# Prompt heads' suffix sums in two rounded parts, a second softplus buffer, and the last value pages in the key buffers

## The reference

```
z = q.k * DH_B**-0.5 + bias
log_stay = where(mask, log_sigmoid(-z), 0)            # minus the softplus of z
after    = suffix sum of log_stay over later keys, without the key itself
w        = where(mask, exp(log_sigmoid(z) + after), 0)
out      = w @ v
```

## Time and profile before

| | |
|---|---|
| runs | 1594.25, 1589.31, 1594.34 us, median 1594.25 |
| profiled execution | 1589.86 us, span 1588.2 us |
| PE busy | 1528.0 us, 96% of the span |
| PE weight loads | 1378.7 us, 87% |
| DVE busy | 1027.7 us, 65% |
| ACT busy | 684.5 us, 43% |
| attention turns | about 258 to 465 us |
| key and value pages | 128 each, 256 KB a page |
| mean TensorE clock | 0.99 of full speed |

### The profile page before, as it was taken

How to read it: one execution, slowest core, us unless ns; L and a number is a source line. 1 busy time by engine, 2 the same in 40 slices (tenths; PEclk the granted TensorE clock), 3 DMA queues, 4 the chain that set the end, 5 groups by cost and what they waited for, 6 DMA issues and landing times.

```text
span 1588.2 us, 31016 instructions
## 1 busy us (share of the span) xinstructions
PE 1528.0 (96%) x12126; PEld 1378.7 (87%) x12126; DVE 1027.7 (65%) x1768; ACT 684.5 (43%) x1029; POOL 94.7 (6%) x173
## 2 busy tenths in 40 slices
PE   7899999999989999999999899999999999999995
PEld 7788987444459999999999889998899999999995
DVE  5555565455553877776667755877758676776665
ACT  5222223645624653344343734354555534344343
POOL 0000002333230000000000000000000000000000
PEclk9999999999999999999999999999999999999997
DMA  5322228898871322222322311223422222222311
GB/s 186 111 74 86 84 72 304 303 353 324 313 277 54 98 88 82 96 69 100 106 79 96 100 57 54 91 100 113 140 80 81 89 83 95 91 71 102 106 54 58
DMA packets 50611, 195.26 MB, mean 123 GB/s; under 512 B 7405, under 2 KB 9614, under 8 KB 36690
## 3 DMA queue, kind: packets, MB, share of 16 engines
q1 hardware_dynamic: 35938, 139.49, 25.9%
q0 software_dynamic: 14576, 54.41, 9.1%
HBM read 182.19 MB, written 11.68 MB: 122 GB/s over the span
## 4 chain that ended last, share of the span: by engine, by line
PE 79%; DVE 11%; ACT 4%; DMA 3%; issue 2%; SPq 1%; POOLq 0%; POOL 0%; ACTq 0%; DVEq 0%
PE ps L333 17%; PE ps L335 16%; PE ps L334 16%; PE ps L738 5%; PE ps L737 5%; PE ps L736 5%; DMA kbuf<-in_k_cache_dram 3%; DVE wlo L322 2%; PE ps L1637 2%; ACT whi L318 1%; SPq L1616 1%; PE ps L1664 1%; PE ps L1872 1%; DVE s0b L2653 1%; PE ps L1830 1%
## 5 line engine op out<-in xcount | busy, mean ns | idle before, releaser
L333 PE MATMUL ps<-xhi,whi 128*128 128x280 f32 x1344 | 402.6, 300 | 23.4 <-DVE wlo L543 10.9
L335 PE MATMUL ps<-xhi,wlo 128*128 128x280 f32 x1344 | 393.7, 293 | 0.0
L334 PE MATMUL ps<-xlo,whi 128*128 128x280 f32 x1344 | 393.6, 293 | 0.0
L333 PE MATMUL ps<-dhi,whi 128*128 128x280 f32 x1024 | 298.4, 291 | 4.7 <-DVE pj L1052 2.9
L335 PE MATMUL ps<-dhi,wlo 128*128 128x280 f32 x1024 | 298.4, 291 | 0.0
L334 PE MATMUL ps<-dlo,whi 128*128 128x280 f32 x1024 | 298.1, 291 | 0.0
L322 DVE TENSOR_TENSOR wlo<-raw,whi 128x2048 fp32r<-128x2048 f32 x97 | 222.1, 2290 | 113.0 <-ACT whi L318 112.6
L318 ACT ACTIVATE whi<-raw 128x2048 fp32r<-128x2048 f32 x96 | 183.3, 1910 | 235.1 <-PE ps L335 201.3
L333 PEld LDWEIGHTS ps<-xhi,whi 128*128 128x128 f32 x1344 | 255.6, 190 | 32.9 <-issue 18.6
L334 PEld LDWEIGHTS ps<-xlo,whi 128*128 128x128 f32 x1344 | 255.5, 190 | 0.5
L335 PEld LDWEIGHTS ps<-xhi,wlo 128*128 128x128 f32 x1344 | 255.3, 190 | 0.0
(11 more groups left out here) (448 smaller groups left out, 2358.5 us busy)
## 6 DMA issues: line engine op xcount, KB each, us to landing
raw<-in_weights_dram SPq DMA_DIRECT2D x98, 1024.0 KB, 4.9
kbuf<-in_k_cache_dram SPq DMA_DIRECT2D x128, 256.0 KB, 5.3
vbuf<-in_v_cache_dram POOLq DMA_DIRECT2D x128, 256.0 KB, 8.5
s0b<-in_gla_in_dram POOLq DMA_DIRECT2D x4, 1024.0 KB, 5.1
out_dram<-s0b POOLq DMA_DIRECT2D x4, 1024.0 KB, 6.8
hT<-in_x_dram SPq DMA_DIRECT2D x2, 1120.0 KB, 9.1
out_dram<-pj POOLq DMA_DIRECT2D x2, 1120.0 KB, 8.9
hT<-in_x_dram POOLq DMA_DIRECT2D x2, 1120.0 KB, 13.6
```

Of the source, the lines that this page charges most:

```text
L333: pe.matmul(out, whi[:, par, t, :], hi, start=first, stop=False)
L334: pe.matmul(out, whi[:, par, t, :], lo, start=False, stop=False)
L335: return pe.matmul(out, wlo[:, par, t, :], hi, start=False, stop=last)
```

## The change

The suffix sums of a prompt head are done on two parts of the softplus: `sph`, rounded to the type `float32r`, made by ScalarE (`phi_act`), and `spl`, the rest `sp - sph` in the same type, made by VectorE (`plo_dve`). PE multiplies each part by the inclusive mask `incl` and by `onesr`, both in that type, with one matmul for every pair of key blocks; the block sums are gone. `sp` and `spl` get a second buffer in a free slot of the low weight parts, so `psp_dve` waits for the head before the last one (`a_v` starts at 1). `sph` lies in the place of `lz`. The last sample's 16 value pages are issued by SyncE into the key buffers (`load_last_v`) after the last `qk_pe`, and GpSimd's loop ends one set earlier; the reload of `hT` now waits for the last `pv_pe` (`v_used` at 36).

```diff
+        vlast = [at(f"vlast{g}", (o_hT, o_hT + GB, o_K2, o_raw)[g], [P, PG, 4 * P]) for g in range(4)]
-        incl = at("incl", o, [P, P]); o += 512
+        incl = at("incl", o, [P, P], f32r); o += 512
+        onesr = at("onesr", o_s + 1184 + 1024, [P, P], f32r)
-        lz = at("lz", o, [P, WA]); o += 4 * WA
-        sp = at("sp", o, [P, WA]); o += 4 * WA
+        lz = at("lz", o, [P, WA])
+        sph = at("sph", o, [P, WA], f32r); o += 4 * WA
+        sps = [at("sp0", o, [P, WA]), at("sp1", o_lo + SLAB * 4, [P, WA])]
+        spl = [at("spl0", o, [P, WA], f32r), at("spl1", o_lo + SLAB * 4, [P, WA], f32r)]; o += 4 * WA
...
+        def load_last_v(sp_, numbers):
+            sp_.wait_ge(S["k_used"], 36)
+            for a in range(PG):
+                for g in range(4):
+                    sp_.dma_start(vlast[a][:, g], page(v_cache, numbers[4 * a + g])).then_inc(KLD[a], 16)
...
-            dve.wait_ge(S["a_sp"], i * 2 + (j + 1))
-            blk = lambda k, q, n=1: sp[:, KOFF[k] + P * (q - k):KOFF[k] + P * (q - k + n)]
-            own.link(dve.tensor_tensor(T_[0], blk(2, 3), blk(3, 3), ALU.add))
-            dve.tensor_tensor(T_[1][:, P:2 * P], blk(1, 3), T_[0], ALU.add)
-            own.link(dve.tensor_tensor(T_[1][:, 0:P], blk(1, 2), blk(2, 2), ALU.add))
-            dve.tensor_tensor(T_[2][:, 0:P], blk(0, 1), blk(1, 1), ALU.add)
-            dve.tensor_tensor(T_[2][:, P:3 * P], blk(0, 2, 2), T_[1], ALU.add).then_inc(S["a_T"], 1)
+        def phi_act(act, i, j):
+            act.wait_ge(S["a_sp"], i * 2 + (j + 1))
+            for r, c in FULL:
+                act.activation(sph[r, c], sps[j % 2][r, c], ACT.Copy).then_inc(S["a_h"], 1)
+        def plo_dve(dve, i, j):
+            for n, (r, c) in enumerate(FULL):
+                dve.wait_ge(S["a_h"], i * 4 + (2 * j + n + 1))
+                dve.tensor_tensor(spl[j % 2][r, c], sps[j % 2][r, c], sph[r, c].bitcast(f32), ALU.subtract)\
+                   .then_inc(S["a_T"], 1)
...
+            for part, (t, ready) in enumerate(((sph, "a_h"), (spl[j % 2], "a_T"))):
+                cols = lambda k, q: t[:, KOFF[k] + P * q:KOFF[k] + WID[k]]
+                pe.wait_ge(S[ready], i * 4 + (2 * j + 1))
+                for k in range(3):
+                    b, c = ZB[k]
+                    if part == 0 and k == 2:
+                        pe.wait_ge(S[ready], i * 4 + (2 * j + 2))
+                    pe.matmul(ps[:, b, c:c + WID[k]], incl[:, :], cols(k, 0), start=part == 0, stop=False)
+                    for n in range(k + 1, 4):
+                        pe.matmul(ps[:, b, c + P * (n - k):c + WID[k]], onesr[:, :], cols(n, 0), start=False,
+                                  stop=part == 1 and n == 3)
+                if part == 0:
+                    pe.matmul(ps[0:N_META, 3, 0:SEQ], incl[0:N_META, 0:N_META], t[0:N_META, META], start=True, stop=False)
+                for n in range(4):
+                    pe.matmul(ps[0:N_META, 3, P * n:SEQ], onesr[:, 0:N_META], cols(n, 0), start=False, stop=False)
...
-            pool.wait_ge(S["k_used"], 36)
+            pool.wait_ge(S["v_used"], 36)
```

More of the change, by code:

```diff
@@ L1661, in pv_pe @@
             for a in range(PG):
-                pe.wait_ge(VLD[a], i * 128 + 64 * (u + 1))
+                if vs is vlast:
+                    pe.wait_ge(KLD[a], 128 * (DEC_B // 2) + 64)
+                else:
+                    pe.wait_ge(VLD[a], i * 128 + 64 * (u + 1))
                 for g in range(4):
-                    mm = pe.matmul(ps[ROWN * g:ROWN * (g + 1), 7, :], lg[:, u % 2, 4 * a + g, :], vbuf[a][:, g, :],
+                    mm = pe.matmul(ps[ROWN * g:ROWN * (g + 1), 7, :], lg[:, u % 2, 4 * a + g, :], vs[a][:, g, :],
                                    start=a == 0, stop=a == PG - 1)
@@ L1807, in psp_dve @@
         def psp_dve(dve, i, j):
+            sp = sps[j % 2]
             if j:
@@ L1821, in psp_dve @@
-            dve.tensor_tensor(T_[2][:, P:3 * P], blk(0, 2, 2), T_[1], ALU.add).then_inc(S["a_T"], 1)
-        def suffixes_pe(pe, i, j):
[L1825 to L1839, removed]
@@ new lines, in suffixes_pe @@
+        def suffixes_pe(pe, i, j):
+            for part, (t, ready) in enumerate(((sph, "a_h"), (spl[j % 2], "a_T"))):
[13 more added lines that the diff above has]
+                    pe.matmul(ps[0:N_META, 3, P * n:SEQ], onesr[:, 0:N_META], cols(n, 0), start=False, stop=False)
+            lo = spl[j % 2]
+            for part, t in enumerate((sph, lo)):
+                if part:
+                    pe.wait_ge(S["a_T"], i * 4 + (2 * j + 2))
+                pe.matmul(ps[:, 2, 2 * P:3 * P], incl[:, :], t[:, KOFF[3]:KOFF[3] + P], start=part == 0, stop=part == 1)
+            for part, t in enumerate((sph, lo)):
+                pe.matmul(ps[0:N_META, 1, 384:400], incl[0:N_META, 0:N_META], t[0:N_META, METAQ],
+                               start=part == 0, stop=part == 1)
+            pe.matmul(ps[0:N_META, 3, 0:SEQ], incl[0:N_META, 0:N_META], lo[0:N_META, META], start=False, stop=True)              .then_inc(S["a_A"], 1)
@@ L1907, in step @@
                     load_k(sp_, i, u + 1, page_numbers(sp_, i, u + 1), range(4))
+                else:
+                    load_last_v(sp_, page_numbers(sp_, DEC_B // 2 - 1, 1))
             later_turns(sp_, step)
@@ L1916, in load_values @@
             step(0, 1)
-            with pool.Fori(1, DEC_B // 2) as i:
+            with pool.Fori(1, DEC_B // 2 - 1) as i:
                 for u in range(2):
                     step(i, u)
+            step(3, 0)
         def ahead_pe(pe, n):
@@ L1944, in ahead_act @@
             elif n == 6:
+                phi_act(act, 0, 0)
                 act.wait_ge(S["mout"], 80)
@@ L1960, in ahead_dve @@
                 dve.tensor_tensor(incl[:, :], ones, strict, ALU.subtract)
+                dve.tensor_copy(onesr[:, :], ones)
                 qs_dve(dve, 0, 0)
@@ L1977, in ahead_dve @@
                 values_dve(dve, 0, 0)
+                plo_dve(dve, 0, 0)
         def attn_pe(pe):
@@ L2004, in step @@
                     tr_pe(pe, i, u + 1)
-                pv_pe(pe, i, u)
+                pv_pe(pe, i, u, vlast if last else vbuf)
             later_turns(pe, step)
@@ L2017, in attn_act @@
             psoft_meta_act(act, 0, 1)
+            phi_act(act, 0, 1)
             page_act(act, 0, 1)
@@ L2039, in attn_dve @@
             psp_dve(dve, 0, 1)
+            plo_dve(dve, 0, 1)
             own_heads_dve(dve, 0, 0)
@@ L2058, in step @@
                     psp_dve(dve, i, u + 1)
+                    plo_dve(dve, i, u + 1)
                 own_heads_dve(dve, i, u)
@@ L2822, in _ @@
         def _(pe):
-            for name, n in (("lo", 2), ("k_used", 4), ("v_used", 4), ("b_ev", 1), ("h_mix", 1), ("a_o", 1)):
+            for name, n in (("lo", 2), ("k_used", 4), ("v_used", 4), ("b_ev", 1), ("h_mix", 1), ("a_o", 1),
+                            ("a_v", 1)):
                 pe.sem_inc(S[name], n)
```

8 lines of the change are left out of this document (4 added, 4 removed).

## The result

The changed kernel takes 1596.23 us (median of 20 runs, 1591.77 to 1601.32), the kernel before 1593.00 us (20 runs beside them, 1586.75 to 1596.78). The ratio is 1.0029, with a 95% interval of 1.0019 to 1.0039: slower by some 4.6 us (the two medians differ by 3.2). The forecast was 1.0 us faster. The time lies inside the range given, but on the other side of no change; slower had been given 0.18.

A forecast was written before the change was run, and what follows sets the result against it. Key-page transfers and PE's own work were taken as nearly equal limits in the attention turns. Terms -0.6 - 0.3 - 0.8 + 0.7 = -1.0 us took 1589.86 to 1588.9, forecast as a median of 1592; range 1583 to 1600.

The forecast's parts named there:

- value pages in the key buffers: End of the attention stage: no gain from the pages, reload of x issued later, delay 0.7 us (0 to 5).
- the cover in the turns: Attention turns: added vector and scalar work ends before the keys land, hidden with under 1 us to spare; otherwise 1.7 us a turn.
- Suffix matmuls: Prompt heads' suffix sums on PE: 4.9 us a head instead of 6.1, saving 1.2 us (0 to 2.1).
- Where it counts: Turns 1 to 6: key landing stays fixed, so PE's saving becomes waiting; 0.3 us gained in all (0 to 1).
- t0: End of a turn's page score matmuls, from which SyncE refills the key buffers; keys arrive 20 to 23 us later.
- Vector and scalar work: Attention turns: block sums go, subtraction (2.1 us) and two copies come; hidden before the keys land, under 1 us to spare.
- Rival C: Vector chain in the turns: L1846 sets the prompt scores (L1776), 1.7 us in five turns, 1597 us; chance 0.08.
- First turn: First attention turn: vector work adds 0.6 us, suffix sums give back 1.2; net -0.6 us (-1.5 to +0.6).
- Last turn: Last attention turn, no keys loaded: L1846 will wait for the page scan until 444.9; gain 0.8 us (0 to 1.5).
- Rival B: Longer PE stalls before the page scores halve the clock, up to 1.7 us each, six times; 1599 us, chance 0.10.
- Rival D: Suffix matmuls: rounded type runs no faster in these shapes, 17 us a head, +11 in eight; chance 0.02.
- E: End of the last value matmuls, 459.8 us; x's reload is issued then and lands 8 to 15 us later.

The follow-up runs named there:

- moving the fetch: Changed kernel without its last part, with unread matmuls in PE's idle time: next pair's head-data fetch moved from VectorE to ScalarE; 1591.06 us, 0.9994.
- shortening the chain: Changed kernel without its last part, with unread matmuls: head-data fetch on ScalarE, main tile masked, copied and split first, all value pages loaded; 1592.73 us, 1.0006.
- the unread matmuls at the first place only: Whole change plus two matmuls with unread results before the first page scores (L1525) in the first turn; ratio 1.0027 to the kernel before.
- The early reload: Whole change, but the reload of x waits only for the last product's first two groups of value pages; 1592.88 us, 1.0005 to the kernel before.
- the last part alone: Kernel before with only the last value pages in the key buffers and x reloaded after the last value matmuls; 1593.50 us, 0.9997.
- the fill without the last part: Changed kernel without its last part, with unread matmuls (two, two, one) before three waits of PE; 1592.23 us, 0.9996 to the kernel before.
- the fill's profile: Profile of the whole changed kernel with unread matmuls (two, three, four) before three waits of PE; 1593.33 us, 1.0000 to the kernel before.
- the kernel without the matmuls of ones: Kernel before without the matmuls of ones in the prompt heads' suffix sums, nothing put in their place; 1589.11 us, 0.9979.

## Why the prediction was wrong

The step that failed for the time is the term for the value pages in the key buffers: a delay of 0.7 us from the quiet row, with nothing for what stands behind the wait. It measured 3.7 us in the profile, and letting x go earlier takes back 3.8 in the runs. A second step, the cover in the turns, failed on the mechanism. Step by step:

*Suffix matmuls: right.* 4.9 us a head, as taken.

*Where it counts: the number right, the reason half right.* The six periods did not change (149.3), as the forecast had it, and the key pages do hold the turns of the kernel before (4 us, shown by half the value pages). But the keys are not alone in holding the changed ones: with half of the value pages the vector chain does, and with all of them the two lie so near each other that moving the fetch (0.9996 to 0.9994) or shortening the chain (1.0006) gains nothing.

*Vector and scalar work: the step that failed on the mechanism.* "In a stalled turn: meta softplus done t0 + 2.6 ... Hidden, with less than 1 us to spare". The chain does not start at t0. It starts at the end of the prompt scores, and its meta softplus ends 8.9 us later, in the changed kernel (280.2 to 289.2) as in the kernel before (279.5 to 288.4). Only where PE stalled for the keys is t0 late enough for 2.6; where PE went straight on, t0 comes some 3.5 us after that start and the softplus is done at about t0 + 5.4 (283.0 and 288.4 before). The slack that I had was the stall, which the change was expected to keep. Rival C described this, with its sign to wait for (L1776, now L1789, waiting for the subtraction), and got 0.08. Its price was wrong the other way: I added it to periods that the keys set, but it lies beside them, and with all pages loaded the runs show no cost of it. This miss explains why nothing was gained, not the loss.

*First turn: -0.6 forecast, +0.8 in the profile.* The added wait was right (0.5 us); the step assumed full rate behind it, since the earlier trace rows kept it after 1.74 us. After 2.25 us it wasn't kept in this execution, and it was in four other profiles: of the 0.8 some 1.1 us is the luck of the profile, without which the step would have come out at -0.3.

*Last turn: -0.8 forecast, +1.0.* "L1846 ... will wait for the page scan" was right, at 446.0. The gain on VectorE's side was 0.5 us from t0 (13.1 instead of 13.7 us) and was lost at half clock. This too is of one execution: with the unread matmuls at the first place only, PE waits the same 2.63 us and the value product behind takes 3.64 us, not 4.32.

*Value pages in the key buffers: 0.7 forecast, 3.7 in the profile.* This term was mis-sized most. I took the landing from a quiet row; it took 10.8 us for its second half. The range of 0 to 5 held it, but I left out what stands behind the wait: PE's 3.40 us, and the clock. The early reload takes back 3.8 us in the runs.

*Rival B, the clock*, had 0.10 and was put at the page scores in the turns. In the changed kernel's profile the mechanism is seen at the three other long waits and not there, where the key waits are 1.6 and 1.0 us. In other profiles it is seen at the page scores as well, the last part alone and the fill without the last part among them: after nine key waits of 2.06 to 4.42 us the scores took 5.1 to 5.3 us, after one of 3.23 and all shorter ones 3.6. I had priced each edit at the full rate, though each of them lengthened a wait that was already near the one that had cost 1.7 us at the earlier trace rows.

*Rival D's sum* is wrong: 17 us a head against 6.1 is +11 for one head, 88 in eight. Its chance of 0.02 and the range did not hang on it.

Open: why the last part alone costs nothing measurable, though its profile has a late x and half clock behind it. Its wait for x was 0.4 us, and the landing of x after E varied from 10.0 to 12.0 us between profiles with the last part (10.4 in that one, 12.0 in the changed kernel's), so a share of luck in either profile can't be excluded. How the 4.6 us divide between late x and clock is not shown: both remedies take back most of the loss, the intervals overlap, and the fill's profile had no wait for x either. And PE can lose its full clock in the page suffix sums without having waited (last section), which no experiment here took away.

## What to carry to other kernels

A chain that crosses engines has to be timed as a round of its own, from the instruction that starts it and not from an event of another limit; slack read in a stalled turn is the stall. Where several limits lie within a microsecond of each other, time taken from one engine comes back as waits, and on PE a longer wait may cost twice, in itself and in the clock behind it. A transfer that shares a buffer should wait for the part it overwrites and not for the whole.

## What the runs showed of the hardware

The spread between runs of one kernel (10 us) goes in good part with the clock: pooled within kernels the correlation of time with mean granted clock is -0.73, 1.25 us for each 0.001 (single kernels: -0.27 to -0.93), so about half of the variance. What one fall of the clock costs is read from rows: the page scores took 5.3 us instead of 3.6, 1.7 us.

The half clock did not follow the waits strictly. Of the PE waits of 2 us and more in these profiles most had half clock behind them. But the four waits of 2.25 us named above did not, nor the key wait of 3.23 us, nor this one, behind which each projection matmul kept its 0.13 us (the kernel filled at the first turn only, behind x):

```profile
476.10 0.40 PE L337 MATMUL ps<-xhi,whi 128*128 128x280 f32 x1 [3.36 <-DVE wlo L326]
```

And six times between 262 and 440 us, in five profiles of kernels with the two-part suffix sums, the half clock came with PE busy and not waiting right ahead of it, each time in the page suffix sums behind the small matmuls of L1686; it did so three times more in the kernel without the matmuls of ones. Two windows of the kernel with the early reload:

```profile
295.00:298.00 3.00, 3.00 (x24) 2.36 (x22) 2.97 (x5) 0.16 (x1) 2.73 (x6) 1.00 1.04 410
299.00:302.00 3.00, 3.00 (x5) 1.03 (x4) 2.96 (x7) 0.00 (x0) 0.76 (x2) 0.53 1.04 391
```

PE is busy throughout, with the suffix sums, the small matmuls of L1686 and the page suffix sums. These took 1.94 and 1.91 us there, 1.12 and 1.02 at full clock, 1.7 us in all. The Trainium skill, "TensorE: Matmul & The Clock Gate", Part 1, explains the half clock by how busy TensorE has been, and warns of idle gaps. By the busy time that the profile counts, 3.00 of 3.00 us ahead of the half clock, these rows don't show the first at work, and the gap alone doesn't tell here when it comes.
